# A hybrid decoder step in fp32: own buffers for x, two-head attention steps, paired 64-row tiles, one table set, and seven products for four in two projections

## The reference, cut to what matters

```python
h = rmsnorm(x, g_pre)
hq, hf, hi, hg, nq, kc, vc, ksl, vsl, kw, vw, ng, mg = split(h @ w_in)
# branch A: 8 heads of a gated linear recurrence, chunks of 32 tokens
logf = log(lb + (1 - lb) * sigmoid(hf));  k = (1 - lb) * sigmoid(-hf)
o_hg = rmsnorm(hgrn2_scan(silu(hq), logf, k, hi, s0), norm_g) * silu(hg)
# branch B: 16 query heads on 4 kv heads of width 64, three kinds of attention
#   (means of 32-token blocks, selected blocks, window of 512), each softmax times a gate
o_nsa = nsa_combine(o_c, o_s, o_w, sigmoid(ng))
u = sigmoid(mg[:, 0]) * o_hg + sigmoid(mg[:, 1]) * o_nsa
x = x + rmsnorm(u @ w_out)
up = rmsnorm(x) @ w_up                    # 1024 -> 5632
c = conv_b + sum_j ext[:, j:j + T] * conv_w[j]      # causal, width 3; ext = history + up
a, b = split(c);  x = x + rmsnorm((silu(a) * b) @ w_down)   # 2816 -> 1024
```

## Time and profile before

| | us |
|---|---|
| median of 3 runs | 2103.85 (2099.66 to 2148.79) |
| profiled execution | 2103.77 |
| its span | 2102.0 |
| TensorE's mean granted clock | 0.935 of full |
| PE, DVE, ACT, POOL busy | 91%, 38%, 28%, 21% |

### The profile page before, as it was taken

The page is one execution under the profiler, slowest core; times in us unless marked ns, Lnnn a source line. Parts: engine busy times, 40 slices in busy tenths (PEclk is TensorE's granted clock), DMA queues, the critical chain, the costliest instruction groups (busy, mean ns, idle before and its releaser), DMA issues.

```text
span 2102.0 us, 25915 instructions
## 1 busy us (share of the span) xinstructions
PE 1921.4 (91%) x9819; PEld 1317.9 (63%) x9819; DVE 789.4 (38%) x1554; ACT 588.3 (28%) x1251; POOL 432.5 (21%) x514
## 2 busy tenths in 40 slices
PE   5999999999979899986888888999799999999996
PEld 4777777777858555553556566774377777763332
DVE  4677776651000345533554452111233333330002
ACT  2222222221001356543444543003411111110103
POOL 2334444421000311135555530000000000000000
PEclk8999999998989589998999999999899999999998
DMA  5766666646320100015677768221322222211111
GB/s 170 260 222 221 214 222 207 223 153 209 60 91 1 41 1 1 1 32 161 207 212 233 239 193 231 76 72 60 85 61 61 60 72 69 61 60 50 60 38 45
DMA packets 201014, 248.82 MB, mean 118 GB/s; under 512 B 32201, under 2 KB 173850, under 8 KB 192538
## 3 DMA queue, kind: packets, MB, share of 16 engines
q1 hardware_dynamic: 176684, 134.16, 21.9%
q0 software_dynamic: 21248, 109.46, 15.2%
q10 hardware_dynamic: 2960, 3.54, 0.5%
HBM read 236.09 MB, written 19.29 MB: 121 GB/s over the span
## 4 chain that ended last, share of the span: by engine, by line
PE 63%; issue 20%; DVE 7%; ACT 4%; DMA 3%; POOL 1%; another core or an unknown queue 1%; ACTq 1%; SPq 1%; POOLq 0%; DVEq 0%
PE ps L1522 14%; PE ps L1969 9%; PE ps L1533 5%; PE ps L1756 5%; PE ps L1843 4%; PE ps L1865 3%; PE ps L1914 3%; DVE mem L1108 3%; PE ps L1554 2%; PE ps L1820 2%; PE ps L1739 2%; PE ps L1768 2%; DMA mem<-in_cache_cmp_kv,pidx 2%; ACT mem L932 1%; PE ps L1625 1%
## 5 line engine op out<-in xcount | busy, mean ns | idle before, releaser
L1522 PE MATMUL ps<-mem 128*128 128x288 f32 x1536 | 401.0, 425 | 20.3 <-DVE mem L1134 18.7
L1522 PEld LDWEIGHTS ps<-mem 128*128 128x128 f32 x1536 | 305.4, 200 | 109.1 <-issue 19.7
L1944 PE MATMUL ps<-mem 128*128 128x288 f32 x1408 | 349.8, 410 | 0.0
L1944 PEld LDWEIGHTS ps<-mem 128*128 128x128 f32 x1408 | 267.3, 191 | 73.1
L680 POOL DMA_INDIRECT mem<-in_cache_sel_kv,sidx x192 | 183.9, 958 | 340.4 <-PE ps L1703 194.1
L1969 PE MATMUL ps<-mem 128*128 128x512 f32 (+1 forms) x440 | 205.3, 611 | 0.0
L1108 DVE TENSOR_TENSOR mem<-mem 128x2048 f32<-128x2048 f32 x56 | 160.0, 2857 | 35.6 <-DMA mem<-in_cache_cmp_kv,pidx 34.8
L1969 PEld LDWEIGHTS ps<-mem 128*128 128x128 f32 (+1 forms) x440 | 72.4, 180 | 132.1 <-issue 132.0
L643 POOL DMA_INDIRECT mem<-in_cache_cmp_kv,pidx x56 | 98.6, 1760 | 265.5 <-DVE mem L1108 243.4
L710 POOL COPY mem<-mem 128x2 f32<-128x2 f32 x44 | 11.3, 256 | 611.5 <-ACT mem L996 611.5
L1865 PE MATMUL ps<-mem 128*64 128x512 f32 x288 | 82.3, 647 | 57.4 <-ACT mem L932 29.6
(11 more groups left out here) (301 smaller groups left out, 2327.1 us busy)
## 6 DMA issues: line engine op xcount, KB each, us to landing
mem<-in_cache_sel_kv SPq DMA_DIRECT2D x320, 128.0 KB
mem<-in_w_up SPq DMA_DIRECT2D x44, 512.0 KB, 5.2
mem<-in_w_in SPq DMA_DIRECT2D x32, 512.0 KB, 3.8
mem<-in_w_in SPq DMA_DIRECT2D x14, 1024.0 KB, 5.2
mem<-in_w_down SPq DMA_DIRECT2D x10, 1024.0 KB, 5.0
mem<-in_state_win_kv SPq DMA_DIRECT2D x16, 512.0 KB
out<-in_state_win_kv POOLq DMA_DIRECT2D x8, 1008.0 KB, 16.0
mem<-in_x_prompt SPq DMA_DIRECT2D x8, 512.0 KB, 6.6
```

Of the source, the lines that this page charges most:

```text
L1522: mm = t.matmul(ps[:, 2 * (u % 2) + a, 0:NHF], lhs(k), hT[:, k, a * NHF:(a + 1) * NHF], start=(k == 0), stop=(k == KD - 1))
L1944: mm = t.matmul(ps[:, 2 * (u % 2) + a, 0:NHF], lhs(k), hT[:, k, a * NHF:(a + 1) * NHF], start=(k == 0), stop=(k == KD - 1))
```

## The change

1. **Start.** x has five buffers and a semaphore each; SP issues x0 and x1, then the parameters, x2 to x4, weight blocks 0 and 1, then the conv parameters and the page table. DVE's constants stand behind the norm tiles. The transposes of the conv parameters are put on PE behind the first unit of head 0.
2. **One table set.** ACT loads the set that holds both Ln and Exp ahead of Ln in each head, ahead of the w_out loop and ahead of the down loop.
3. **K/V rows.** Two blocks share five units; the fifth has both blocks' 64 sample rows, in column halves.
4. **Prompt attention.** 64 steps of two heads, e = 0 and 1:

```diff
-        UNITS = [(i, h + e, br) for i in range(PT) for h in range(0, NH, 2) for br in range(2) for e in range(2)]
-        TLAG, VLAG = 4, 7
+        STEPS = [(i, gp, r, br) for i in range(PT) for gp in range(2) for r in range(R) for br in range(2)]
+        TLAG, VLAG = 2, 3
...
+                b = 2 * (n % 2)
+                wait(pe, p_ok, n - 1)
+                for e in range(2):
+                    t.matmul(ps[:, b + e, i * P:w], identb[:, :], penb[:, :], start=True, stop=False, skip_group_check=True)
+                for e in range(2):
+                    mm = t.matmul(ps[:, b + e, 0:w], nqT[64 * e:64 * e + 64, 4 * gp + r, i * P:w], kT[64 * e:64 * e + 64, br, gp, 0:w],
+                                  start=False, stop=True, skip_group_check=True)
```

```diff
+                g.tensor_tensor(s1w[j % 2], a21, a22, ALU.add).then_inc(sw_s, 1)
+                g.tensor_tensor(s2w[j % 2], s1w[j % 2], a11, ALU.subtract).then_inc(sw_s, 1)
+                g.tensor_tensor(a21, a11, a21, ALU.subtract).then_inc(sw_s, 1)
+                g.tensor_tensor(s4w, wquads(B_UP + j)[1], s2w[j % 2], ALU.subtract).then_inc(sw_s, 1)
...
+                product(0, a11, b11, True, pp)
+                product(1, s2w[j % 2], tw[1], True, pp)
+                product(2, s1w[j % 2], tw[0], True, pp)
+                product(0, a12, b21, False, pp)
+                product(1, s3w, tw[2], False, pp)
+                product(3, a22, tw[3], True, pp)
+                product(2, s4w, b22, False, pp)
...
+                for o, x, y in zip(u2, n1_parts(p1), n1_parts(p6)):
+                gated(j - 1)
+                v.tensor_tensor(u3, p1, p6, ALU.add).then_inc(up_v, 1)
+                for o, x, y in zip(c22, n1_parts(u3), n1_parts(p5)):
+                v.tensor_tensor(u3, u3, p4, ALU.add).then_inc(up_v, 1)
+                for o, y in zip(u2, n1_parts(p5)):
```

7. **w_out and down.** The tail tile's two 512-column halves (in down, two of 256) go to the two column halves of the array; ACT copies them out of PSUM ahead of the square:

```diff
+                steps = [(a, k) for a in range(2) for k in order] if i < PT else [(a, k) for k in order for a in range(2)]
+                    out = ps[:, 2 * w + a, :] if i < PT else ps[64 * a:64 * a + S, 2 * w, :]
...
+                            for e in range(2):
+                                mm = t.matmul(ps[64 * e:64 * e + S, bank, 0:256], gT[:, k, T:N], ws[:, k - k0, 256 * e:256 * e + 256],
```

More of the change, by code:

```diff
@@ L59 @@
 U_KV = 4 * HH
[L60 removed]
+U_KT = U_KV + 15
 U_CM = U_KT + 4
@@ L189, in build @@
         at[0] = a_h
-        xt = [view(D) for _ in range(2)]
+        xt = [view(D) for _ in range(TT)]
         xn = [view(D) for _ in range(2)]
@@ L1641, in kv_unit @@
             def kv_unit(u):
[L1642 to L1645 removed]
+                p, k = divmod(u - U_KV, 5)
+                if k < 4:
+                    b = B_KV + 2 * p + k // 2
+                    if k % 2 == 0:
+                        weights(b)
+                    rows(u, k % 2, b)
+                    return
+                banks_free(u)
+                w = [wslot[(B_KV + 2 * p + e) % NSLOT].rearrange("p (k c) -> p k c", c=WB) for e in range(2)]
+                for j in range(KD):
+                    for e in range(2):
+                        mm = t.matmul(ps[64 * e:64 * e + S, 2 * (u % 2), 0:WB], hT[:, j, T:N], w[e][:, j, :],
+                                      start=(j == 0), stop=(j == KD - 1))
+                mm.then_inc(proj, 1)
             pe.wait_ge(hT_ok, TT)
@@ L1897, in _, with swap, product @@
-            pe.wait_ge(u_hT, 2 * KD)
+            def swap():
+                pe.wait_ge(eo_ok, SB)
+                heads = ident[:, :].rearrange("p (k e t) -> p k e t", e=2, t=ST)
+                for b in range(SB):
+                    for e in range(2):
+                        mm = t.matmul(ps[64 * e:64 * e + 64, 7, b * S:(b + 1) * S], osb[:, b, :], heads[:, :, e, :], start=True, stop=True)
+                mm.then_inc(sw_ok, 1)
+            def product(bank, lhs, rhs, first, count):
+                for k in range(KD // 2):
+                    mm = t.matmul(ps[:, bank, 0:NHF], lhs[:, k, :], rhs[:, k, :], start=(first and k == 0),
+                                  stop=(k == KD // 2 - 1), skip_group_check=True)
+                mm.then_inc(count, 1)
@@ new lines, in _ @@
+            b11, b12, b21, b22 = hquads()
+            pe.wait_ge(ekT_ok, SB * (NPC + 1))
+            pe.wait_ge(esc_ok, NC * SB)
+            for q in range(KD):
+                weights(B_MG + q)
+                a11, a12, s3m, a22 = wquads(B_MG + q)
+                wait(pe, mg_a, 2 * q)
+                product(0, a11, b11, True, mp)
+                pe.wait_ge(ms_ok, 4 * q + 2)
+                pe.wait_ge(mt_ok, 1)
+                wait(pe, mg_v, 5 * (q - 1) + 2)
+                product(1, s2m[q % 2], mtw[1], True, mp)
+                wait(pe, mg_v, 5 * (q - 1) + 5)
+                product(2, s1m[q % 2], mtw[0], True, mp)
+                pe.wait_ge(mg_a, 2 * q + 1)
+                product(0, a12, b21, False, mp)
+                pe.wait_ge(ms_ok, 4 * q + 3)
+                pe.wait_ge(mt_ok, 2)
+                pe.wait_ge(mg_v, 5 * q + 1)
+                product(1, s3m, mtw[2], False, mp)
+                wait(pe, mg_v, 5 * (q - 1) + 4)
+                product(3, a22, mtw[3], True, mp)
+                pe.wait_ge(ms_ok, 4 * q + 4)
+                pe.wait_ge(mg_v, 5 * q + 3)
+                product(2, s4m, b22, False, mp)
+                if q == 0:
+                    swap()
```

688 lines of the change are left out of this document (432 added, 256 removed).

## The result

The changed kernel takes **1938.8 us** (median of 4 runs, 1931.9 to 1943.7); the ratio to the kernel before is **0.922** (interval 0.917 to 0.927), where 1949 was predicted, a ratio of 0.926. The profiled execution took 1931.9, its span is 1930.1, 171.9 under the 2102.0 of before.

What follows compares the result with a forecast made beforehand. The prediction took PE, busy 91% of the span, as the bound. Its terms for the stages summed to -155 us, from 2103.8 to 1949; likeliest 1932 to 1968 (0.50), range 1920 to 2000.

Steps and rivals of the forecast that it cites:

- H, up: Up projection: seven products of four matmuls, block from 16.16 to 14.0 us, 5 us of stalls allowed: -41.7 us.
- the port: Up: DVE and POOL block each other at a shared SBUF port, 0.8 us per block, +18 us; within the likeliest case.
- the second rival: Merge and up blocks: each product start costs 0.2 us at six joints of 30 blocks, +36 us, 1985; chance 0.14.
- D, prompt attention: Prompt attention: two scores overlap on row groups, shorter steps give -41 us, less 8 for a longer low clock: -33.
- the first rival: Prompt attention: the two scores don't overlap, only saved switches remain, -10 us for -33, 1972 in all; chance 0.12.
- The third rival: Prompt attention: the clock stays low through the whole stage, +55 us, 2004 in all; chance 0.07.
- A, start: Start: with own buffers the five x tiles land one behind the other some 12 us in: -13 us taken.
- B, heads: HGRN heads: one table set removes loads of 1.28 us, one per head, ahead of a DVE add: -9 us.
- E, handover: Handover to merge: swap and copy leave the path, weights ahead of V cost 1 to 5 us: 0 taken.
- G, w_out: w_out and norms: tail tile in column halves -6.9 us, four table loads -5.1, two copies +1.1: -11 taken.
- I, down: Down projection: tail tile in two column halves -17 us, shorter end and earlier first tile -4.4.
- The slower rival: Merge and up: the clock falls to half in the block products, up to +410 us, 2359 in all; chance 0.03.

Runs made afterwards that it cites:

- e3: Changed kernel with POOL's four weight sums per up block left out from the third block on: up stage 309.6 us for 309.2.
- e2: Changed kernel with an eighth, unread product of four matmuls in each of the 22 up blocks: up stage 352.05 us, 42.85 more.
- e1: Changed kernel with each head's mask product right ahead of its scores, so the two scores aren't neighbours: prompt attention 276.4 us, 67 more.
- c1: The kernel before, unchanged, profiled again on another chip: 2136.7 us, prompt attention 284.3 instead of 247.8.
- e7: Changed kernel with two buffers for x by turns again, its issue order kept: PE's first projection starts at 23.8 us, for 18.6.
- e4: Changed kernel without the one table set loaded ahead of Ln in the heads: heads stage 413.2 us for 402.4.
- c2: The changed kernel again, unedited, as a control: median 1936.5 us, ratio 0.922 to the kernel before.
- e5: Changed kernel without the one table set loaded ahead of the w_out and down loops: w_out 86.0 us for 77.2, down 204.9 for 201.3.
- e6: Changed kernel with down's 64-row tail tile computed by one matmul of 512 columns again: down stage 217.7 us for 201.3.
- e9: Changed kernel with V loads before gate weights, K/V row DMAs between query copies, w_out weights awaited by block, early up T sums: median 1917.6 us.

## Why the prediction was right

The sum, 1949, was 10 above the median and 17 above the profiled execution; the range held it. By its steps:

- **H, up,** missed most: -50.7 for -41.7. Of the 9 us, 4 are the block (13.80, not 14.0), and 5 the stalls allowed for, of which there were none between blocks. The dates of the chain held, and the port, which was weighed at 0.8 a block on the path, took 3.5 a block off it (e3). Seven products take 13.58 (1656.41 to 1669.99), 28 x 0.485, so that nothing is left for the starts of six more: the second rival is refuted. Of the block's 2.36 a product is 1.95 (e2); 0.23 were the two history transposes that stood before each block (1601.65 to 1601.88 in the trace of before) and now stand ahead of the stage.
- **D, prompt attention:** -38.7 for -33. The mechanism was right (e1): the scores overlap, the first rival is refuted. The step that failed is the allowance for a longer low clock. The changed kernel was at 1.2 GHz from 639 to about 700, 61 us, and not 25 us longer than the 74 of before. The single steps missed both ways, and that they sum to the -41 is luck: in the last tile a step takes 3.49 for 3.65, but in the first, at half clock, 2.52 (2.30 and 2.73 by turns) for 2.2. From first mask to first mask the first tile took 52.1 for 57.9, 5.8 less where 12.5 were forecast. The third rival, the clock staying low, happened to the kernel before (c1) and to e1, but in no profile of the changed order.
- **A, start:** -16.9 for -14. The chain per tile was right; "land one behind the other some 12 us in" failed. x0 is issued first and squared at 6.1, so the order of issue, not the buffers, was the larger part (e7).
- **B, heads:** -11.2 for -8 net, and about -7 if the means of the profiles are set against each other. The number is near by luck. The step that failed is "7 x 1.28 = 9": the waits shrank by about 3 us in the mean (19 to 16), so of the 9 about 3 were on the path; most of the rest is the clock, which no term had and which isn't shown to be the tables' doing (e4, c1).
- **C, K/V rows:** -13.0 for -10.5, within the scatter of that stage (121 to 128 among the profiles of after).
- **E, handover:** +8.2 for 0 in the first profile, and +0.4 in c2. The bound of 5 us for weights ahead of V was too small: PE waits 9 to 10 for the last windows, where it waited 2.4 for V's pages before.
- **F, merge:** -14.2 for -15.1. The wait for w_out stayed, as said.
- **G, w_out:** -11.0 for -11, by a sum whose parts hang together otherwise: with the paired tail the tables are worth 8.6 (e5).
- **I, down:** -22.0 for -21.4; 16.4 the tail (e6), 3.5 the tables (e5); the other 2.1 fit the earlier first tile, which no run tests.
- The slower rival, the clock falling in the block products, didn't come: 1.00 in merge and 0.99 in up.

Queries and gates gave 3.2 by no edit: 72.8 or 76.0 is a matter of the clock, 0.97 or 0.93, in either kernel. So errors of both signs lay within the total: 13 us of stalls and clock allowance that were not needed and a clock that helped in two stages, against the first tile's 7 and the 8 of the sample attention.

## What to carry to other kernels

Where PE is busy all the time, count its columns: seven products for eight gave seven eighths, and 104 us of sums on POOL cost nothing as long as each result has a date that it meets with a few us to spare. Ask for each queue what an early piece of work pushes back: in e9 sums of DVE, put ahead of an urgent copy, cost 6 us, and weights ahead of V made PE wait 9 to 10. And compare a stage at the same granted clock before its change is put down to an edit: the heads' stage differs by 4 us between two executions of the kernel before. Before a slow first product is put down to a wait, look at the granted clock of that window.

## What was not expected of the hardware

- Two 64-row products on different row groups overlap fully as neighbours (1.13 for four records against 1.12 for two), and a 128-row bf16 product between them ends it.
- One stage of the kernel before can stay at 1.2 GHz for its first 73 or its first 157 us in executions of the same code, with PE busy nearly all of both, and take 37 us longer; with the new order of steps it was 59 to 66 us in each of eleven profiles. What sets the length is not shown.
- 104 us of sums on POOL lengthened DVE's work by 71 us over the stage, with no effect on the time, while 52 us of small copies on POOL beside DVE's taps lengthened those by nothing (0.83 each).
- One chip ran the sample attention in 327 to 330 us, others in 363 to 387, for nearly the same code. What differs between the chips was not tried and stays open.
